# Channel products in two blocks of passes per unit, and a two-layer model's end by token tile

## What is computed

```
h = rmsnorm(x, g_ffn[l])
u = causal_dwconv(h @ w_up[l], ffn_conv_w[l]) + ffn_conv_b[l]
gate, val = jnp.split(u, 2, axis=-1)
x = x + (jax.nn.silu(gate) * val) @ w_down[l]
...
return rmsnorm(x, g_final)
```

## Time and profile before

| | |
|---|---|
| median of three runs | 1980.49 us (1979.66 to 1981.14) |
| the profiled execution's own time | 1980.04 us |
| its span | 1978.2 us |
| granted TensorE clock, mean over the span | 0.997 |
| TensorE busy | 1953.9 us, 99% of the span, 9884 matmuls |
| weight loads busy (beside matmuls) | 1643.8 us, 83% |
| VectorE busy | 1287.4 us, 65% |
| ScalarE busy | 1028.3 us, 52% |

### The profile page before, as it was taken

The page is one execution under the profiler, slowest core; times in us unless marked ns, Lnnn a source line. Parts: engine busy times, 40 slices in busy tenths (PEclk is TensorE's granted clock), DMA queues, the critical chain, the costliest instruction groups (busy, mean ns, idle before and its releaser), DMA issues.

```text
span 1978.2 us, 28715 instructions
## 1 busy us (share of the span) xinstructions
PE 1953.9 (99%) x9884; PEld 1643.8 (83%) x9884; DVE 1287.4 (65%) x1793; ACT 1028.3 (52%) x1498; POOL 46.2 (2%) x74
## 2 busy tenths in 40 slices
PE   8999999999999999999999999999999999999997
PEld 6788888888888888888888888888888888888886
DVE  6644675656644675655767766877787787754453
ACT  5533576664433576664544444555555555534442
POOL 1000030000000020000100000000000000000000
PEclk9999999999999999999999999999999999999998
DMA  8666545545566545545666455556555565565553
GB/s 284 209 194 191 145 148 157 159 150 188 184 194 192 149 149 173 158 153 186 207 191 189 152 167 181 184 183 188 185 186 184 187 187 184 188 215 192 192 194 124
DMA packets 245638, 357.29 MB, mean 181 GB/s; under 512 B 15239, under 2 KB 134369, under 8 KB 245021
## 3 DMA queue, kind: packets, MB, share of 16 engines
q1 hardware_dynamic: 243916, 349.35, 56.6%
q0 software_dynamic: 1616, 6.61, 1.0%
HBM read 352.75 MB, written 3.16 MB: 180 GB/s over the span
## 4 chain that ended last, share of the span: by engine, by line
PE 98%; DVE 1%; DMA 0%; issue 0%; ACT 0%; SPq 0%; DVEq 0%; ACTq 0%
PE acc L348 20%; PE acc L326 19%; PE acc L328 19%; PE acc L327 19%; PE acc L347 10%; PE aux L403 2%; PE acc L344 1%; PE acc L345 1%; PE aux L804 1%; PE aux L785 1%; PE aux L822 1%; PE aux L821 1%; DMA sb_kz<-mem 0%; PE aux L793 0%; PE aux L792 0%
## 5 line engine op out<-in xcount | busy, mean ns | idle before, releaser
L304 DVE TENSOR_TENSOR sb_w_lo<-sb_stage,sb_w_hi 128x1024 fp32r<-128x1024 f32 x656 | 800.5, 1223 | 521.3 <-ACT sb_w_hi L299 513.3
L299 ACT ACTIVATE sb_w_hi<-sb_stage 128x1024 fp32r<-128x1024 f32 x656 | 690.8, 1056 | 637.9 <-PE acc L328 365.7
L348 PE MATMUL acc<-sb_xT,sb_w_hi 128*128 128x512 f32 x1740 | 616.8, 398 | 0.0
L347 PE MATMUL acc<-sb_xT,sb_w_lo 128*128 128x256 f32 x1740 | 490.3, 282 | 0.0
L348 PEld LDWEIGHTS acc<-sb_xT,sb_w_hi 128*128 128x128 f32 x1740 | 327.0, 188 | 77.5
L347 PEld LDWEIGHTS acc<-sb_xT,sb_w_lo 128*128 128x128 f32 x1740 | 328.7, 189 | 2.6
L326 PE MATMUL acc<-sb_w_hi,sb_xT 128*128 128x512 f32 x768 | 306.2, 399 | 0.3 <-issue 0.3
L328 PE MATMUL acc<-sb_w_hi,sb_xT 128*128 128x512 f32 x768 | 299.5, 390 | 0.0
L327 PE MATMUL acc<-sb_w_lo,sb_xT 128*128 128x512 f32 x768 | 299.3, 390 | 0.0
L326 PE MATMUL acc<-sb_w_hi,sb_mT 128*128 128x512 f32 x560 | 225.2, 402 | 0.0
L328 PE MATMUL acc<-sb_w_hi,sb_mT 128*128 128x512 f32 x560 | 218.9, 391 | 0.0
(11 more groups left out here) (251 smaller groups left out, 1573.7 us busy)
## 6 DMA issues: line engine op xcount, KB each, us to landing
sb_stage<-w_in SPq DMA_DIRECT2D x248, 512.0 KB, 3.9
sb_stage<-w_up SPq DMA_DIRECT2D x176, 512.0 KB, 3.5
sb_stage<-w_out SPq DMA_DIRECT2D x96, 512.0 KB, 3.7
sb_stage<-w_down SPq DMA_DIRECT2D x88, 512.0 KB, 3.6
sb_stage<-w_kv SPq DMA_DIRECT2D x16, 512.0 KB, 5.6
sb_stage<-w_ukv SPq DMA_DIRECT2D x16, 512.0 KB, 3.6
sb_stage<-w_uq SPq DMA_DIRECT2D x12, 512.0 KB, 3.6
sb_kz<-mem SPq DMA_DIRECT2D x4, 512.0 KB, 9.9
```

The costliest lines, as they stand in the source:

```text
L299: act.activation(w_hi[:, j % RING, 0:size], stage[:, j % RING, 0:size], ACT.Copy).then_inc(hi_ready, 1)
L304: dve.tensor_tensor(w_lo[:, j % RING, 0:size], stage[:, j % RING, 0:size], w_hi[:, j % RING, 0:size].bitcast(F32), ALU.subtract).then_inc( ...
L347: pe.matmul(o[:, 0:SEQ], lo[:, k, cols], xT[:, k0 + k, 0, :], start=False, stop=False)
L348: mm = pe.matmul(o, hi[:, k, cols], both, start=False, stop=last and k == 3)
```

## The change

In the channel products the 16 matmuls of a unit stay the same, but their order becomes: all 8 short passes, then all 8 long ones. In the first unit of a chunk it is all 8 long ones, then all 8 short ones.

At the end, the last four units of the last chunk (as many as the ring holds) are multiplied for token tile 0 first, through all four units, and then for token tile 1; each tile raises a semaphore of its own. The final norm goes by token tile: add, square, `rstd` of that tile alone, scale, store. Of each tile ScalarE scales the channels up to 1024, VectorE the next 512 and then the last 512 with the gain; the stores are two per tile, of 1024 channels each, tile 0 first.

```diff
--- before.py
+++ after.py
@@ -258,6 +258,7 @@
         xo_hi, xo_lo = sem("xo_hi"), sem("xo_lo")
         sum_ready, tap2_done = sem("sum_ready"), sem("tap2_done")
         gate_conv, gate_silu, act_ready = sem("gate_conv"), sem("gate_silu"), sem("act_ready")
+        last_product = [sem("last_product0"), sem("last_product1")]
         last_added, final_rstd = sem("last_added"), sem("final_rstd")
         final_last = [sem("final_last0"), sem("final_last1")]
         gain_applied, final_row = sem("gain_applied"), [sem("final_row0"), sem("final_row1")]
@@ -335,17 +336,27 @@
             slot = j % RING
             hi = w_hi[:, slot, :].rearrange("p (k n) -> p k n", n=256)
             lo = w_lo[:, slot, :].rearrange("p (k n) -> p k n", n=256)
-            for k in range(4):
-                both = xT[:, k0 + k, :, :].rearrange("p h t -> p (h t)")
-                for c in range(2):
-                    o = acc[:, 2 * pair + c, :]
-                    cols = slice(c * P, (c + 1) * P)
-                    if first and k == 0:
-                        pe.matmul(o, hi[:, k, cols], both, start=True, stop=False)
-                        mm = pe.matmul(o[:, 0:SEQ], lo[:, k, cols], xT[:, k0 + k, 0, :], start=False, stop=False)
-                    else:
-                        pe.matmul(o[:, 0:SEQ], lo[:, k, cols], xT[:, k0 + k, 0, :], start=False, stop=False)
-                        mm = pe.matmul(o, hi[:, k, cols], both, start=False, stop=last and k == 3)
+            tiles = [(k, c) for k in range(4) for c in range(2)]
+
+            def rest_passes():
+                for k, c in tiles:
+                    mm = pe.matmul(acc[:, 2 * pair + c, 0:SEQ], lo[:, k, c * P:(c + 1) * P], xT[:, k0 + k, 0, :],
+                                   start=False, stop=False)
+                return mm
+
+            def main_passes():
+                for k, c in tiles:
+                    both = xT[:, k0 + k, :, :].rearrange("p h t -> p (h t)")
+                    mm = pe.matmul(acc[:, 2 * pair + c, :], hi[:, k, c * P:(c + 1) * P], both,
+                                   start=first and k == 0, stop=last and k == 3)
+                return mm
+
+            if first:
+                main_passes()
+                mm = rest_passes()
+            else:
+                rest_passes()
+                mm = main_passes()
             mm.then_inc(unit_used, 1)
 
         def product_rope_key(pe, base, j, k0, first, last):
@@ -625,8 +636,8 @@
                     for i in range(FT // 2):
                         load(sp, U4, (FT // 2) * c + i, w_down2[:, 2 * i:2 * i + 2, c * 512:(c + 1) * 512], 512)
 
-                for ready, cols in ((final_row, slice(0, 3 * 512)), (final_last, slice(3 * 512, D))):
-                    for t in range(T):
+                for t in range(T):
+                    for ready, cols in ((final_row, slice(0, 2 * 512)), (final_last, slice(2 * 512, D))):
                         sp.wait_ge(ready[t], 1)
                         sp.dma_start(by_token(out)[:, t, cols], x[:, t, cols]).then_inc(stored, 16)
                 sp.wait_ge(stored, 64)
@@ -1083,10 +1094,24 @@
 
                 for c in range(4):
                     banks_free(pe, PAIRS4, c)
-                    for i in range(FT // 2):
+                    for i in range(FT // 2 - (RING if c == 3 else 0)):
                         if c == 0:
                             pe.wait_ge(act_ready, i + 1)
                         product_rows(pe, U4, (FT // 2) * c + i, act_T, 2 * i, 2, 512, c % 2, i == 0, i == FT // 2 - 1)
+                for t in range(T):
+                    o = acc[:, 2 + t, :]
+                    for i in range(FT // 2 - RING, FT // 2):
+                        j = (FT // 2) * 3 + i
+                        pe.wait_ge(lo_ready, U4 + (j + 1))
+                        hi = w_hi[:, j % RING, :].rearrange("p (k n) -> p k n", n=512)
+                        lo = w_lo[:, j % RING, :].rearrange("p (k n) -> p k n", n=512)
+                        for k in range(2):
+                            a_hi = act_T[:, 2 * i + k, 0, t * P:(t + 1) * P]
+                            a_lo = act_T[:, 2 * i + k, 1, t * P:(t + 1) * P]
+                            pe.matmul(o, a_hi, hi[:, k, :], start=False, stop=False)
+                            pe.matmul(o, a_hi, lo[:, k, :], start=False, stop=False)
+                            mm = pe.matmul(o, a_lo, hi[:, k, :], start=False, stop=(i, k) == (FT // 2 - 1, 1))
+                    mm.then_inc(last_product[t], 1)
 
 
             @block.scalar
@@ -1385,9 +1410,9 @@
                 for t in range(T):
                     act.wait_ge(last_added, t + 1)
                     x_step(act.activation(junk[:, :], x[:, t, 3 * 512:D], ACT.Square, accum_out=sumsq_x[:, t, 3:4]))
-                act.wait_ge(final_rstd, 1)
-                act.activation(x[:, 1, 0:3 * 512], x[:, 1, 0:3 * 512], ACT.Copy, scale=rstd[:, 1:2])\
-                   .then_inc(final_row[1], 1)
+                    act.wait_ge(final_rstd, t + 1)
+                    act.activation(x[:, t, 0:2 * 512], x[:, t, 0:2 * 512], ACT.Copy, scale=rstd[:, t:t + 1])\
+                       .then_inc(final_row[t], 1)
 
 
             @block.vector
@@ -1900,16 +1925,16 @@
                     if c < 3:
                         add_to_x(dve, U4, (FT // 2) * (c + 1) - 1, c % 2, c)
 
-                multiplied(dve, U4, U_DOWN - 1)
-                last = slice(3 * 512, D)
+                dve.wait_ge(gain_applied, 3)
+                third, last = slice(2 * 512, 3 * 512), slice(3 * 512, D)
                 for t in range(T):
+                    dve.wait_ge(last_product[t], 1)
                     dve.tensor_tensor(x[:, t, last], acc[:, 2 + t, :], x[:, t, last], ALU.add).then_inc(last_added, 1)
-                dve.wait_ge(gain_applied, 3)
-                x_rstd(step, dve, SQ_PRO * (4 + LAYERS), final_rstd)
-                dve.wait_ge(final_rstd, 1)
-                dve.tensor_scalar(x[:, 0, 0:3 * 512], x[:, 0, 0:3 * 512], rstd[:, 0:1], None, ALU.mult)\
-                   .then_inc(final_row[0], 1)
-                for t in range(T):
+                    dve.wait_ge(x_squared, SQ_PRO * (3 + LAYERS) + 6 + t + 1)
+                    step(dve.tensor_reduce(sumsq2[:, t:t + 1], sumsq_x[:, t, :], AX_X, ALU.add))
+                    rsqrt(step, dve, rstd[:, t:t + 1], sumsq2[:, t:t + 1], 1, D, final_rstd)
+                    dve.wait_ge(final_rstd, t + 1)
+                    dve.tensor_scalar(x[:, t, third], x[:, t, third], rstd[:, t:t + 1], None, ALU.mult)
                     dve.scalar_tensor_tensor(out=x[:, t, last], in0=x[:, t, last], scalar=rstd[:, t:t + 1],
                                              in1=gfin[:, last], op0=ALU.mult, op1=ALU.mult).then_inc(final_last[t], 1)
 
```

## The result

| | before | after |
|---|---|---|
| median of the runs | 1980.82 us (1979.66 to 1982.1, 4 runs) | 1969.82 us (1969.39 to 1970.43, 4 runs) |
| the profiled execution | 1980.04 us | 1970.00 us |
| its span | 1978.2 us | 1968.2 us |
| start of the last matmul | 1964.86 us | 1958.50 us |
| from there to the end of the span | 13.3 us | 9.7 us |

The ratio of after to before is 0.9946, with a 95% interval of 0.9935 to 0.9958: 8.3 to 12.9 us faster. The median moved by 11.0 and the profiled execution by 10.0.

The account below looks back on a forecast made before the run. The prediction took TensorE, through the cost of each matmul, as the bound. The pass order's 10.3 us plus the end's 2.9 made 13.2 us saved, 1967.3 us; its own range was 1963 to 1972, the wider one 1956 to 1975.

Parts of the forecast that it names:

- A short behind a short, 0.12: In the channel products, a short pass following another short was taken to cost 0.12 us; break-even 0.126 us.
- Rival A: Channel products: shorts behind shorts run at their stream's rate, 0.113 us; 25.0 us saved in all, 1955.5 us; chance 0.14.
- Rival C: Channel products: weight loads bound the short run, slower kernel; 2082 us at 0.188 us per short; chance 0.08.
- The new chunk, 11.11 us: A chunk of four units in the new order was forecast at 11.11 us against 11.29, 0.178 us saved.
- 29 x 0.2267: In the new chunk, 29 longs following a long were counted at 0.2267 us each, 6.574 us together.
- The channel products, 10.3 us: Saving from the new pass order over all 58 chunks, 0.178 us each: 10.3 us.
- The last four units: no wait: Last 48 matmuls, tile 0 first: weights ready with 1.5 us margin, tile 0's norm beside tile 1's matmuls with 0.4.
- The end, 2.9 us: After the last matmul, tile 1's shorter norm chain and the half-sized remaining store were to save 2.9 us.
- Sum: Whole kernel: 10.3 us from the pass order plus 2.9 from the end, 13.2 us saved, giving 1967.3 us.
- Rival B: Channel products: the new order gives nothing; only the end's 2.9 us remain, 1977.6 us; chance 0.14.
- rival D: End of kernel: order gains as forecast, but tile 0's norm or store runs into tile 1's; 1970.2 us; chance 0.04.
- The gap rule: Channel products: N / 2.4 + 2.5 ns per matmul, 325 ns for a pair in any order, so no gain from order.

Follow-up runs that it names:

- `weights64`: Changed kernel with short passes loading 64 of their 128 weight columns, so half of the output channels is left out: 1960.73 us.
- `short128`: Changed kernel with short passes streaming 128 of the 256 tokens, part of the product left out: 1959.83 us.
- `order_only`: Kernel before with the new order of the passes and the old end: 1973.96 us against 1980.57, ratio 0.9965.
- `tail_only`: Changed kernel with the old order of the passes, keeping the new end: 1977.14 us against 1980.57, ratio 0.9982.
- `short320`: Changed kernel with short passes streaming 320 columns in place of 256, 64 columns the product doesn't ask for: 2019.24 us.
- `alternate`: Changed kernel, but the third unit of a chunk also runs its longs first: 1968.45 us, ratio 0.9938 to the kernel before.
- `runs_of_2`: Changed kernel, but units behind a chunk's first run two shorts, two longs, four times: 1968.99 us against 1983.75 for the kernel before.
- `two_units`: `alternate`, with passes grouped over two units at a time in turns 2 to 22 of the up-projection: 1967.39 us, ratio 0.9939 to the kernel before.
- `runs_of_4`: Changed kernel, but units behind a chunk's first run four shorts, four longs, twice: 1972.69 us against 1983.75 for the kernel before.

## Why the prediction was right, and where it was off

**The bound.** Right: TensorE is busy throughout and VectorE went to 80%.

**A short behind a short, 0.12.** Right to the rounding, and right to take it from the one such place in a chunk. Rival A (0.113) had the stream's rate right, as `weights64` shows, but a short with a full load does not reach it. Rival C's 0.188 was the listed duration of a load, and a load in a row costs 0.11, by `short128`.

**The new chunk, 11.11 us.** Off: it takes 11.15. The term that failed is "29 x 0.2267": the prediction charged the surplus to the one long that stands behind a short, 0.008 us, and counted every later one at the down-projection's price. The surplus is 0.026 us per change, over five longs, three times per chunk: 3 x (0.026 - 0.007) = 0.057 us more. Against it, the first short behind a long takes 0.113 and not 0.1185, 3 x 0.005 = 0.016 less. 11.11 + 0.057 - 0.016 = 11.15. The channel products before had two longs in a row only behind a single short (where a chunk begins), so their rows could not show this. The prediction also took the old chunk's pair of 0.353 us as the cost of its order, while the same order runs at 0.347 in a few chunks; no row of it shows why. The range was drawn for an uncertain short and not for this, and it was luck that it was wide enough.

**The channel products, 10.3 us.** Measured: an undisturbed chunk went from 11.29 to 11.15 us, 0.133 by starts read to the nanosecond. Summed over the 58 chunks, some with other matmuls between, the two traces differ by 7.0 us. `order_only` gave 6.6 us, with an interval from 4.2 to 9.7. So two thirds of the forecast came.

**The last four units: no wait.** Right. No gap stands in TensorE's last stretch, and tile 0's norm fits with 0.42 us to spare where 0.4 was worked out.

**The end, 2.9 us.** Measured 13.3 - 9.7 = 3.6 in the traces and 3.4 by `tail_only`. The compute was right: both engines done 5.4 us behind the last matmul's start, forecast 1970.4 - 1964.86 = 5.5. The term that was too small is the store's: from the end of the compute to the end of the span it took 9.7 - 5.4 = 4.3 us, where 1975.3 - 1970.4 = 4.9 had been taken. The issues took 0.33 to 0.43 us each and the landings 3.1 us at the median, in place of the 3.6 of a 512 KB load; the prediction's other reckoning, by bandwidth (3.4 us saved), was the nearer one.

**Sum.** 7.0 + 3.6 = 10.6 us in the traces' own parts, of which the span shows 10.0: the last matmul came 6.4 us earlier and not 7.0. The part ahead of the channel products, which the change does not touch, was 0.6 us longer in this execution. The two errors, 3.3 us too much and 0.7 too little, partly cancelled, so the sum came out nearer than its larger term did. Rival B (order without effect) falls by `order_only`, whose interval leaves out 1; rival D falls by `tail_only`, whose interval leaves out 1 too. The gap rule of the Trainium skill's section "Back-to-back issue gap", which the prediction set beside its rows, is given there for one matmul by itself, so the 353 ns of a pair in a row is no clean test of it.

## What to carry to other kernels

Where TensorE is always busy, read distances between starts, sorted by what stands before each matmul: one mean per line hides a cost of the neighbourhood. Look at every chunk and not at one, since the same order can have two paces. Grouping passes of unlike length, and letting one unit end with the kind that the next begins with, paid here; but try the length of the runs, for four in a row was worse here than two or eight. A norm behind the last product can be cut by row tile, so that all but the last tile's norm and store lie under matmuls; what is left is one tile's chain.

## What was not expected

In the kernels with 256-column shorts, and in `short320`, the first five 512-column passes behind 8 or more shorts take some 233, 236, 228, 233 and 231 ns (the first 231 to 234) before they return to 227. What in TensorE or its reads causes it stays open. For the kernel's own short pass the runs here exclude late weight loads, the order of the PSUM banks and the number of shorts from eight up.

All these costs come in whole steps. Averaged over the undisturbed chunks from the up-projection's second turn on, a chunk takes 11286.6 ns in the kernel before, 11153.3 in the changed kernel, 11133.3 in `alternate` and `runs_of_2`, 11113.3 in `two_units`, 11213.3 in `runs_of_4`, 10960.0 in `short128`, 12006.6 in `short320`. To 0.1 ns these are 1693, 1673, 1670, 1667, 1682, 1644 and 1801 times 6.667 ns. A long in a row is 34 such steps, a short 18 and with 64 weight columns 17, a short of 320 columns 22 where its share of a long would be 21.25, and the old order's pair is 53 steps in the slow pace and 52 in the quick one. No run here shows where the step comes from.

Open are also why runs of four are worse than runs of two, and what brings the old order into its quick pace.
